# A state-space layer run over pairs of tokens, two tiles to an instruction, with its tables formed during the down product

## What is computed

```python
bu_re = einsum('bsgh,gph->sbgp', u, bb_re)        # u: 256 tokens x 64 groups of 16 channels
bu_im = einsum('bsgh,gph->sbgp', u, bb_im)        # 64 states in a group
s = associative_scan(_ssm_combine, (lambda, bu))  # s[t] = lambda * s[t-1] + bu[t], complex
y = (einsum('sbgp,ghp->bsgh', s_re, c_re) - einsum('sbgp,ghp->bsgh', s_im, c_im)
     + d * u)
y = gelu(y)
return y * sigmoid(y @ w_glu + b_glu)
```

## Time and profile before

| | us |
|---|---|
| median of three runs (3683.43 to 3694.46) | 3687.44 |
| the profiled execution | 3684.38 |
| its span, first to last instruction | 3682.6 |
| TensorE busy | 3449.0 (94%) |
| VectorE busy | 2059.2 (56%) |
| ScalarE busy | 1629.0 (44%) |
| GpSimd busy | 326.1 (9%) |

### The profile page before, as it was taken

The page is one execution under the profiler, slowest core; times in us unless marked ns, Lnnn a source line. Parts: engine busy times, 40 slices in busy tenths (PEclk is TensorE's granted clock), DMA queues, the critical chain, the costliest instruction groups (busy, mean ns, idle before and its releaser), DMA issues.

```text
span 3682.6 us, 43122 instructions
## 1 busy us (share of the span) xinstructions
PE 3449.0 (94%) x15476; PEld 2811.2 (76%) x15476; DVE 2059.2 (56%) x2525; ACT 1629.0 (44%) x2020; POOL 326.1 (9%) x350
## 2 busy tenths in 40 slices
PE   8999999978878899999999979999998999999997
PEld 7888888866665678888888758877777777888775
DVE  5455455469977645444554464565555575445555
ACT  5444444431236635444443464443444545544333
POOL 0000003187750000000000000000000000000000
PEclk9999999988889999999999989999999999999998
DMA  7666665543337656666665665543534653466543
GB/s 225 188 188 190 182 189 188 184 140 92 86 100 229 208 157 182 188 188 189 179 195 187 216 204 157 170 143 123 169 116 138 176 159 103 138 194 203 175 147 126
DMA packets 318564, 618.00 MB, mean 168 GB/s; under 512 B 19216, under 2 KB 27680, under 8 KB 317520
## 3 DMA queue, kind: packets, MB, share of 16 engines
q1 hardware_dynamic: 316160, 606.25, 54.1%
q0 software_dynamic: 2256, 9.78, 0.8%
HBM read 613.86 MB, written 2.10 MB: 167 GB/s over the span
## 4 chain that ended last, share of the span: by engine, by line
PE 78%; DVE 11%; ACT 4%; DMA 3%; POOL 2%; issue 2%; SPq 0%; ACTq 0%; DVEq 0%; POOLq 0%
PE acc L249 19%; PE acc L250 19%; PE acc L251 19%; DVE w_lo L217 4%; DMA w_raw<-in_w_mod 2%; PE pst L644 2%; PE acc L642 2%; PE pst L642 2%; PE acc L643 2%; PE acc L644 2%; PE pst L643 2%; ACT w_hi L211 2%; DVE st_z L1113 1%; PE pst L2076 1%; PE pst L2058 1%
## 5 line engine op out<-in xcount | busy, mean ns | idle before, releaser
L217 DVE TENSOR_TENSOR w_lo<-w_raw,w_hi 128x1024 fp32r<-128x1024 f32 x1160 | 1436.3, 1244 | 1356.7 <-ACT w_hi L211 1336.5
L211 ACT ACTIVATE w_hi<-w_raw 128x1024 fp32r<-128x1024 f32 x1160 | 1223.5, 1059 | 1685.0 <-PE acc L251 1297.7
L249 PE MATMUL acc<-w_hi,act_hi 128*128 128x512 f32 (+1 forms) x3552 | 1421.6, 400 | 25.4 <-DVE w_lo L217 21.6
L250 PE MATMUL acc<-w_lo,act_hi 128*128 128x512 f32 (+1 forms) x3552 | 1396.9, 393 | 0.0
L251 PE MATMUL acc<-w_hi,act_lo 128*128 128x512 f32 (+1 forms) x3552 | 1396.0, 393 | 0.0
L249 PEld LDWEIGHTS acc<-w_hi,act_hi 128*128 128x128 f32 x3552 | 682.0, 192 | 167.5 <-DVE w_lo L217 17.5
L251 PEld LDWEIGHTS acc<-w_hi,act_lo 128*128 128x128 f32 x3552 | 679.6, 191 | 141.4
L250 PEld LDWEIGHTS acc<-w_lo,act_hi 128*128 128x128 f32 x3552 | 681.6, 192 | 133.4 <-issue 0.5
L642 PE MATMUL acc<-w_hi,g_hi 128*128 128x512 f32 x344 | 136.3, 396 | 0.0
L642 PE MATMUL pst<-w_hi,g_hi 128*128 128x512 f32 x344 | 136.2, 396 | 0.0
L643 PE MATMUL pst<-w_lo,g_hi 128*128 128x512 f32 x344 | 136.1, 396 | 0.0
(11 more groups left out here) (380 smaller groups left out, 2480.9 us busy)
## 6 DMA issues: line engine op xcount, KB each, us to landing
w_raw<-in_w_in SPq DMA_DIRECT2D x400, 512.0 KB, 3.7
w_raw<-in_ffn_w_down SPq DMA_DIRECT2D x168, 512.0 KB, 3.8
w_raw<-in_ffn_w_gate SPq DMA_DIRECT2D x160, 512.0 KB, 3.6
w_raw<-in_ffn_w_up SPq DMA_DIRECT2D x160, 512.0 KB, 3.6
w_raw<-in_w_mod SPq DMA_DIRECT2D x96, 512.0 KB, 4.8
w_raw<-in_w_out SPq DMA_DIRECT2D x64, 512.0 KB, 4.4
w_raw<-in_w_branch_a SPq DMA_DIRECT2D x32, 512.0 KB, 4.0
w_raw<-in_w_branch_b SPq DMA_DIRECT2D x32, 512.0 KB, 3.9
```

Of the source, the lines that this page charges most:

```text
L211: act.activation(w_hi[:, s % SLOTS, :], w_raw[:, s % SLOTS, :], ACT.Copy).then_inc(w_hi_done, 1)
L217: dve.tensor_tensor(w_lo[:, s % SLOTS, :], w_raw[:, s % SLOTS, :], w_hi[:, s % SLOTS, :].bitcast(F32), ALU.subtract).then_inc(w_lo_done, 1)
L249: pe.matmul(o, xh, wh, start=k == 0, stop=False)
L250: pe.matmul(o, xh, wl, start=False, stop=False)
```

## The change

Two tokens are taken at a time: the scan runs over 128 pairs, so one frame is the whole tile, the factor is the square of the old one (`MAG2`) and the rotation that of two steps (`COS2`, `SIN2`). The input of a pair is B times the second token plus lambda B times the first (`lb_re`, `lb_im`), and the first token's output is C lambda times the state of the pair before plus a direct term (`cl_re`, `cl_im`, `direct`). These tables are new. GpSimd forms them during the down product, TensorE transposes B there (`state_b_turn_pe`) and forms the direct terms (`direct_terms_pe`), and lambda B is turned back in `w_u` (`lam_b_turn_pe`). u is stored with even tokens ahead of odd ones.

Two tiles make a unit, 16 units in all: an instruction of VectorE or GpSimd holds 128 pairs of two tiles. TensorE forms outputs with channels on the partitions (`ssm_output_pe`), where they are gelu'd by ScalarE during `w_qkv` and need no transposing as input of `glu`; they are transposed for what comes behind (`y_turn_pe`). The steps begin ten chunks later (`SSM_SKIP`), and only then is there a wait for the rotation. Apart from this, the sums of squares of the row norms move from ScalarE (`rows_squares_act`) to VectorE (`rows_stats_dve`, 512 columns each, bn_stats), and the parameters are begun in ffn1.

```diff
@@ state-space steps @@
+        UNITS = ST // 2
+        OUT_LAG = 2
+        SSM_STEPS = UNITS + OUT_LAG
+        SSM_SKIP = 10
...
+        def ssm_input_pe(pe, u):
+            if u >= 2:
+                pe.wait_ge(ssm_b_read, u - 1)
+            j = 32 * (u % 4)
+            for t in range(2):
+                c = 2 * (u // 4) + t
+                for part, (lb, b) in enumerate(((lb_re, b_re), (lb_im, b_im))):
+                    o = pst[:, u % 2, (2 * part + t) * FRAME:(2 * part + t + 1) * FRAME]
+                    pe.matmul(o, lb[j:j + 32, c, :], u_t[j:j + 32, c, 0:FRAME], start=True, stop=False)
+                    mm = pe.matmul(o, b[j:j + 32, c, :], u_t[j:j + 32, c, FRAME:SEQ], start=False, stop=True)
             mm.then_inc(ssm_b, 1)
 
+        def ssm_output_pe(pe, o):
+            pe.wait_ge(ssm_s, o + 1)
+            if o % 4 == 0 and o:
+                pe.wait_ge(ssm_gelu, o // 2)
+            s, j = st_s[:, o % 2], 32 * (o % 4)
+            for t in range(2):
+                c = 2 * (o // 4) + t
+                i, y = 4 * c + o % 4, pst[j:j + 32, 2 + t, :]
+                pe.matmul(y[:, 0:FRAME], direct[j:j + 32, 0, c, :], u_t[j:j + 32, c, 0:FRAME], start=True, stop=False)
+                pe.matmul(y[:, 1:FRAME], cl_re[:, i, :], s[:, 0, t, 0:FRAME - 1], start=False, stop=False)
+                pe.matmul(y[:, 1:FRAME], cl_im[:, i, :], s[:, 1, t, 0:FRAME - 1], start=False, stop=True)
+                pe.matmul(y[:, FRAME:SEQ], direct[j:j + 32, 1, c, :], u_t[j:j + 32, c, FRAME:SEQ], start=True, stop=False)
+                pe.matmul(y[:, FRAME:SEQ], cf_re[:, i, :], s[:, 0, t, :], start=False, stop=False)
+                mm = pe.matmul(y[:, FRAME:SEQ], cf_im[:, i, :], s[:, 1, t, :], start=False, stop=True)
+            mm.then_inc(ssm_y_done, 1)
+
         def ssm_step_pe(pe, i):
-            if i + 1 < ST:
-                ssm_input_pe(pe, i + 1)
+            if i + 2 < UNITS:
+                ssm_input_pe(pe, i + 2)
             o = i - OUT_LAG
...
+            steps.did(dve.tensor_tensor(z[:, 0], b[:, 0], co, M))
+            steps.did(dve.tensor_tensor(z[:, 1], b[:, 1], co, M))
+            steps.settle()
+            steps.did(dve.tensor_tensor(b[:, 1], b[:, 1], si, M))
+            steps.did(dve.tensor_tensor(b[:, 0], b[:, 0], si, M))
+            steps.settle()
+            steps.did(dve.tensor_tensor(z[:, 0], z[:, 0], b[:, 1], A_))
+            steps.did(dve.tensor_tensor(z[:, 1], z[:, 1], b[:, 0], S))
+            steps.settle()
+            dve.sem_inc(ssm_b_read, 1)
...
                 pool.wait_ge(ssm_z, i + 1)
-                if i >= 3:
-                    pool.wait_ge(ssm_y_done, i - 2)
...
+                if i >= 2:
+                    pool.wait_ge(ssm_y_done, i - 1)
@@ down product and w_u @@
+                    if q == 1 and chained and j in (8, 12):
+                        state_b_turn_pe(pe, j // 12, p0)
+                    if q == 1 and chained and j == DOWN_CHUNKS - 6:
+                        direct_terms_pe(pe, p0)
+                    if q == 2 and chained and j == 0:
+                        pe.wait_ge(direct_stored, 1)
...
+        def direct_terms_pe(pe, p0):
+
+            pe.wait_ge(cf_ready, 1)
+            pe.wait_ge(bs_stored, 4)
+            pe.wait_ge(d_ready, 16)
+            pe.matmul(acc[:, 1, 1, 0:8], d_rows[:], ident[0:8, 0:8], start=True, stop=True)
+            for c in range(8):
+                for part, (b, cf) in enumerate(((bs_re, cf_re), (bs_im, cf_im))):
+                    for j in range(4):
+                        mm = pe.matmul(acc[32 * j:32 * j + 32, 1, 0, 32 * c:32 * c + 32], b[:, 4 * c + j, :],
+                                       cf[:, 4 * c + j, :], start=part == 0, stop=part == 1)
+            mm.then_inc(direct_prod, 1)
...
+        def lam_b_turn_pe(pe, half):
+            pe.wait_ge(lam_b, 1)
+            if half:
+                pe.wait_ge(lam_b_stored, 2)
...
@@ programs of ScalarE and TensorE @@
+            stream_split(act, "w_qkv", fetch_prj(act, prj), spread(ssm_step_act, act, SSM_STEPS, "w_qkv", skip=SSM_SKIP))
+            act.wait_ge(ssm_gelu, 8)
+            act.wait_ge(w_used, AT["glu"][0])
+            for n in range(4):
+                y_hi_act(act, n)
+            turn_qku_fetch(act, 0, 4, 12, lambda o, i: act.activation(o, i, ACT.Copy))
+            y_store(act, 0, lambda o, i: act.activation(o, i, ACT.Copy))
             mod_act(act, 0)
...
+            stream_pe(pe, "w_qkv", between=spread(ssm_step_pe, pe, SSM_STEPS, "w_qkv", skip=SSM_SKIP))
+            pe.wait_ge(ssm_gelu, 8)
             turn_qku_pe(pe, 4, 12, "glu")
+            y_turn_pe(pe)
+            stream_pe(pe, "glu", turning=StateOutputs(pe))
```

More of the change, by code:

```diff
@@ L826, in turn_qku_pe @@
                 pe.wait_ge(fetched[m], AT[after][1] + 1)
-            for n, (dst, col, t) in list(enumerate(TQ))[first:last]:
+            for n, (dst, src, col, t) in list(enumerate(TQ))[first:last]:
                 if n >= 4:
@@ new lines, in ssm_params_pool @@
+            pool.sem_inc(lam_c, 1)
+            pool.wait_ge(direct_prod, 1)
+            for g in range(8):
+                t = slice(g * n, (g + 1) * n)
+                lr, li = (par_[:, v, t].unsqueeze(2).broadcast_to(wide) for v in (LRE, LIM))
+                re, im = bs_re[:, t, :], bs_im[:, t, :]
+                tt(cf_tmp[:, 0], im, li, M)
+                tt(cf_tmp[:, 1], re, li, M)
+                steps.settle()
+                tt(re, re, lr, M)
+                tt(im, im, lr, M)
+                steps.settle()
+                tt(re, re, cf_tmp[:, 0], S)
+                tt(im, im, cf_tmp[:, 1], A_)
+                steps.settle()
@@ L1021, in ssm_tables_pool, with lam_b_store_act @@
+        def lam_b_store_act(act, half):
+            act.wait_ge(lam_b_turned, half + 1)
+            for part, b in enumerate((lb_re, lb_im)):
+                act.activation(b[:, 4 * half:4 * half + 4, :], pst[:, 2 + part, :].rearrange("p (c s) -> p c s", c=4),
+                               ACT.Copy).then_inc(lam_b_stored, 1)
         def ssm_tables_pool(pool, steps):
@@ new lines, in ssm_step_act @@
+        def ssm_step_act(act, i):
+            if i == 0:
+                act.wait_ge(tables_ready, 1)
+            o = i - OUT_LAG
+            if 0 <= o < UNITS and o % 4 == 3:
+                act.wait_ge(ssm_y_done, o + 1)
+                for t in range(2):
+                    act.activation(u_t[:, 2 * (o // 4) + t, :].rearrange("p (s two) -> p two s", two=2),
+                                   pst[:, 2 + t, 0:SEQ].rearrange("p (two s) -> p two s", two=2),
+                                   ACT.Gelu_apprx_tanh).then_inc(ssm_gelu, 1)
```

391 lines of the change are left out of this document (223 added, 168 removed).

## The result

The changed kernel takes 3716.4 us (median of four runs, 3715.3 to 3718.2) where the kernel before takes 3688.0 in the runs beside it (3683.4 to 3694.5): 1.0074 times as long, 95% interval 1.0061 to 1.0086. It was forecast 12 us faster; it is 28 us slower, and outside the range. The profiled execution has a span of 3716.3 us against 3682.6, 33.7 more.

A forecast was written before the change was run, and what follows sets the result against it. VectorE, with GpSimd on the same beat, was taken to bound the `w_qkv` state-space steps. From 3684.4 us, -15 (`w_qkv`), -6 (behind it) and +9 (ahead) gave 3672, put down as 3674 for the runs' median; range 3642 to 3708.

The forecast's parts named there:

- What bounds the kernel: In the state-space steps inside `w_qkv`, VectorE sets the pace, 7.8 us a tile, with GpSimd on the same beat.
- The state work: TensorE's input and output matmuls in `w_qkv`: 5.7 us a unit (2.6 inputs, 3.0 outputs), 91 us for 16 units.
- The new wait: In `w_qkv`, TensorE's input matmuls wait for VectorE's products of the same step: 2.5 us for 14 units, 35 us.
- The clock: In `w_qkv`, half clock after each TensorE wait loses 1.4 us, 20 in all, range 0 to 48.
- the signs to look for: In `w_qkv`: some 14 waits of 2.2 to 2.6 us, inputs 2.6, outputs 3.0, stage 277 us, clock 0.9.
- Rival 1: In `w_qkv`, the clock falls after every wait; wait and lost clock reach 6.3 us a unit: 3708, slower, chance 0.16.
- Rival 2: In `w_qkv`, state matmuls are cheap, 0.21 us each, 4.4 a unit, with half the clock loss: 3643, chance 0.2.
- Rival 3: In `w_qkv`, each change of tile shape costs 0.09 us, 8 a unit, 12 us: 3686, no change, chance 0.1.
- Rivals 4 and 5: Late tables make `w_u` wait on lambda B, 3694, chance 0.02; VectorE still bounds `w_qkv`, stage 275 us, chance 0.04.
- The work ahead: Ahead of `w_qkv`, 32 transposes cost TensorE 3 us and the 64 direct-term matmuls 6 us: 9 us more.
- The tail: From the end of `w_qkv` to `mod`, 39.6 us before: 11.5 from last output to `glu`, 6 us gained (2 to 8).
- The sum: Whole kernel: 15 us less in `w_qkv`, 6 less behind it, 9 more ahead of it, together 12 us faster.

The follow-up runs named there:

- in two parts and with paired strips: Changed kernel with inputs issued one chunk ahead of outputs, no wait, direct terms grouped, and neighbouring tiles on different strips made a unit: 3585.4 us, 0.972 of the kernel before.

## Why the prediction was wrong

**What bounds the kernel: right.** VectorE left the critical path: 34% busy over the steps. A step of VectorE is what I took, in its timeline of the changed kernel:

```profile
899.28 1.23 DVE L222 TENSOR_TENSOR w_lo<-w_raw,w_hi 128x1024 fp32r<-128x1024 f32 x1 [11.72 <-ACT w_hi L216]
900.42 0.42 DVE L1261 TENSOR_TENSOR st_z<-pst,rot_cos 128x256 f32<-128x256 f32 x1
...
902.90 1.37 DVE L1275 TENSOR_TENSOR_SCAN st_z<-ssm_par,st_z 128x128 f32<-128x128 f32 x4
```

2.48 us from the first product to the scans (I took 2.35), 1.3 for the scans.

**The state work: right in the sum.** 88 us against 91. The inputs were cheaper than put (1.98 for 2.6), the outputs dearer (3.53 for 3.0). The inputs run close to the pace of 128 rows; what costs in the outputs is the change of the weights' shape.

**The new wait: right.** 14 waits of 2.05 us, where 2.2 to 2.6 were to show. Its mechanism was as told: VectorE makes the rest of a chunk (899.28), then its products, and TensorE stands at the input matmuls from the end of its chunk until 902.87. GpSimd didn't hold `w_lo` up, which was the 0.4 too much.

**The clock: the step that failed.** The prediction put "1.4 us for each, 20 in all" and kept 0 to 3.4 a wait. Measured: 5.3 for each of the 12 waits with outputs and 1.7 for the two without, 67 us behind the 14 waits. The term was mis-sized by 47 us, and that is more than the whole miss of 42. Two errors are in it.

The first is what stood behind the wait. The term was priced from rows of the kernel before, in which a wait stood in front of 2 us of state work; the change put 5.5 us of narrow matmuls there, and with those the loss is not 1.7 to 3.4 but 4.6 to 6.2. The half clock lay on the state work too, 6.20 us for 3.53, which the signs to look for (outputs in 3.0 us) left out.

The second is which rows were taken. The trace of the kernel before has more waits than those three. Beside the 2.42 us of the earlier trace rows (and one of 2.48 with a second wait right behind it), the nearest in size to the 2.2 to 2.6 forecast are four of 2.91 to 2.95. The windows behind them:

```profile
861.70:871.70 10.00, 9.96 (x36) 7.55 (x36) 9.77 (x19) 1.06 (x1) 7.62 (x9) 0.66 0.39 114
916.20:926.20 10.00, 9.94 (x36) 7.53 (x36) 9.76 (x20) 1.06 (x1) 7.63 (x9) 0.66 0.39 113
939.80:949.80 10.00, 9.63 (x41) 7.48 (x42) 9.79 (x19) 1.06 (x1) 7.62 (x9) 0.83 0.39 110
1018.80:1028.80 10.00, 10.00 (x37) 7.59 (x37) 9.79 (x19) 1.06 (x1) 7.62 (x9) 0.66 0.37 112
```

They lose 3.4, 3.4, 1.7 and 3.4 us, 3.0 on the mean and 2.7 with the 2.42: 38 to 42 us for 14 waits, and a forecast of 3692 to 3696, no gain. The other 20 to 24 us of the miss are the first error. The two rows that seemed to show a limit (1.39 us of wait did nothing, 1.44 did) showed none: a wait of 0.46 lost up to 4.6.

**The rivals.** Rival 1 was what happened: its point of decision, wait and lost clock together over 4.8 us a unit, was passed with 7.3. Its price (6.3, 3708) was low for the same reason, and its chance, 0.16, rested on the wait of 1.39 us. Rival 2 (cheap matmuls) is half right: where the shape stays, a matmul took 0.22 us, near its 0.21, but with the changes of shape a unit is 5.5 and not 4.4; only neighbours on different strips brought it below that (2.9). Rival 3 is half right as well: a change of shape costs 0.12 at full clock (9 us for five of them in each unit). The price of the outputs held a part of that, 3.0 us where twelve at 0.22 are 2.6 and 3.53 were measured. It didn't show in the row that I held against it; why it doesn't there, no run tells. The Trainium skill, "TensorEngine Tiling (Array Packing)", Key Properties, says that a change of mode drains TensorE; the runs agree, at this price. Rivals 4 and 5 did not come: TensorE waits for nothing new in the down product and `w_u`.

**The work ahead: right, by a cancellation.** In TensorE's timeline of the changed kernel, the down product, a group of eight transposes takes 0.79 us (578.36 to 579.15), four are 3.2. The direct terms take 1.2 us (602.90 to 604.13), not 6:

```profile
578.36 1.04 PE L1097 MATMUL acc<-ident_sb,b_re 128*128 128x128 f32 x8
579.15 0.47 PE L657 MATMUL pst<-w_hi,g_hi 128*128 128x512 f32 x1
```

```profile
602.59 0.38 PE L1111 MATMUL acc<-ident_sb,d_rows 8*128 8x8 f32 x2
602.90 0.27 PE L1115 MATMUL acc<-cf_re,bs_re 128*32 128x32 f32 x8
...
604.13 0.50 PE L657 MATMUL pst<-w_hi,g_hi 128*128 128x512 f32 x1
```

That is 0.02 us for a matmul of 32 columns on 128 rows, where one alone took 0.23. The same section of the Trainium skill says that different tiles of the array work in parallel; the runs agree, and my sentence on it was still too high (4 us), since it divided the price of lone matmuls by four. The two prices are 4.4 of the 7 us. Some 1 us more is a longer stop right ahead of the first input (2.47 us against 1.55), and some 2 are not located. The sum came out near because a term put too high stood beside one left out, which is luck.

**The tail: right.** From the last output to `glu` 11 us, to `mod` 32.7 in place of 39.6, in TensorE's timeline of the changed kernel:

```profile
1122.61 5.15 PE L855 MATMUL pst<-ident_sb,prj 128*128 128x128 f32 x32 [3.05 <-ACT prj L836]
1128.63 1.94 PE L1313 MATMUL pst<-ident_sb,u_t 128*128 128x128 f32 x16 [0.88 <-DVE k_t L867]
...
1130.33 0.47 PE L254 MATMUL acc<-w_hi,act_hi 128*128 128x512 f32 x1
...
1152.21 0.39 PE L1513 MATMUL acc<-w_hi,act_hi 128*128 128x512 f32 x1
```

**The sum**, once more: -7 in the tail, +7 ahead, +32 in `w_qkv`. That is 32 of the 33.7 us by which the span grew. The change as such is a gain: with the same work and the waits covered it is 0.985 of the kernel before, in two parts and with paired strips 0.972.

## What to carry to other kernels

Price a wait of TensorE by the matmuls that stand behind it, at half clock, and not by the wait alone: here 2 us of waiting cost 7.3, and moving two lines, so that work which is ready comes before work that waits, gave back 82 us. Keep narrow matmuls in short runs between full ones (2 to 3 us here kept the clock, 5.5 did not always), keep matmuls of one shape together, and let neighbours go to different strips of the array, where two then took the time of one. A clock price read off another place of the trace failed here, where other work stood behind the wait; and it is safer to read every wait of that size in the trace than three of them.

## What the runs showed of the hardware

- Lost clock came in amounts of about 1.6, 3.1, 4.7 and 6.2 us a step and hardly anything between, whatever the length of the wait.
- Without any wait, 5.5 us of narrow matmuls between two chunks were followed by 3.4 us at 1.2 GHz in four of twelve steps (the kernel with the outputs first), and brought 6.8 us of it in two steps with the inputs one step later; 2 and 3 us apart from each other never did, in twelve steps.
- Narrow matmuls can bring half clock without any wait. In `w_out` the changed kernel runs 32 fp32 matmuls of two columns in a row, with no wait before or in them; a window from 1356.8 to 1361 reads 1.00, one from 1361.2 to 1371.2 reads 0.50. The kernel before has the same matmuls and reads the same there (1.00 from 1323.4 to 1327, 0.50 from 1327.3 to 1337.3):

```profile
1356.78 9.67 PE L1525 MATMUL pst<-pick,mod_nat 128*128 128x2 f32 x64
```

- At full clock a matmul of 128 columns took 0.22 to 0.25 us on 32 rows, on 128 rows into 32 columns of the array too; a change between these shapes added 0.07 to 0.12. On two different strips, two took 0.24 together; 64 of 32 columns round four strips took 1.2.
- Four scans of 128 columns took 1.37 us in a row with GpSimd idle, under my low bound of 1.6 (four times the shortest in the earlier trace rows).
